# Sixteen transfers of eight partitions for part of a weight load

## The reference

```python
def expert_choice_ffn(h, router_w, wg, wu, wd):
    B, S, D = h.shape
    C = max(1, EC_CAPACITY_FACTOR * S // N_EXPERTS)          # 32 tokens per expert
    aff = jax.nn.softmax((h @ router_w).astype(jnp.float32), axis=-1)
    gate, idx = lax.top_k(jnp.swapaxes(aff, 1, 2), C)
    ...
    a = jnp.einsum('becd,edf->becf', xs, wg)                  # 1024 -> 1408
    u = jnp.einsum('becd,edf->becf', xs, wu)                  # 1024 -> 1408
    o = jnp.einsum('becf,efd->becd', jax.nn.silu(a) * u, wd) * gate[..., None]
    return jax.vmap(lambda oi, ii: jnp.zeros((S, D), h.dtype).at[ii].add(oi))(o, flat_idx)
```

## Time and profile before

| | |
|---|---|
| median of 3 runs | 1959.3 us (1957.9 to 1959.34) |
| span of the profiled execution (first to last instruction) | 1954.0 us |
| median less that span | 5.3 us |
| TensorE busy | 1562.5 us, 80% of the span |
| mean rate of the DMA engines | 330 GB/s over the span |

### The profile page before, as it was taken

The page is one execution under the profiler, slowest core; times in us unless marked ns, Lnnn a source line. Parts: engine busy times, 40 slices in busy tenths (PEclk is TensorE's granted clock), DMA queues, the critical chain, the costliest instruction groups (busy, mean ns, idle before and its releaser), DMA issues.

```text
span 1954.0 us, 22376 instructions
## 1 busy us (share of the span) xinstructions
PE 1562.5 (80%) x9738; PEld 877.7 (45%) x9738; DVE 561.0 (29%) x1102; ACT 251.6 (13%) x582; POOL 45.8 (2%) x24
## 2 busy tenths in 40 slices
PE   9999999886656675568899999998857566566767
PEld 6687688432222232223365887884313222222323
DVE  3654782211211121123335456612111111111211
ACT  3333210200000000001122432102000000000000
POOL 0300100000000000000003000000000000000000
PEclk9999999987887788789999999999988778877889
DMA  7622046699999999999972224277999999999998
GB/s 301 233 91 87 1 199 242 275 392 430 426 434 429 434 430 432 438 429 422 427 328 87 92 107 184 103 305 310 431 432 438 433 427 428 436 430 435 428 431 365
DMA packets 28221, 643.87 MB, mean 330 GB/s; under 512 B 3040, under 2 KB 4576, under 8 KB 7392
## 3 DMA queue, kind: packets, MB, share of 16 engines
q1 hardware_dynamic: 26960, 638.41, 77.5%
q10 hardware_dynamic: 1168, 4.07, 0.5%
HBM read 641.42 MB, written 1.05 MB: 329 GB/s over the span
## 4 chain that ended last, share of the span: by engine, by line
PE 51%; DMA 45%; DVE 2%; issue 1%; DVEq 1%; ACT 0%; SPq 0%; ACTq 0%
DMA region<-w_down_dram 42%; PE ps L1046 11%; PE ps L630 7%; PE ps L693 6%; PE ps L800 6%; PE ps L866 3%; PE ps L973 2%; DMA ring<-w_gbu_dram 2%; PE ps L656 2%; PE ps L783 1%; PE ps L716 1%; PE ps L671 1%; PE ps L772 1%; DMA region<-w_down_last_dram 1%; PE ps L535 1%; PE ps L598 1%
## 5 line engine op out<-in xcount | busy, mean ns | idle before, releaser
L973 PE MATMUL ps<-ring,region 128*32 128x384 f32 (+1 forms) x2842 | 288.3, 536 | 173.9 <-DMA ring<-w_gbu_dram 173.9
L1046 PE MATMUL ps<-region,late 128*32 128x512 f32 x1320 | 219.7, 790 | 146.7 <-DMA region<-w_down_dram 143.0
L973 PEld LDWEIGHTS ps<-ring,region 128*32 128x32 f32 x2842 | 117.8, 124 | 336.5 <-DMA ring<-w_gbu_dram 192.9
L1046 PEld LDWEIGHTS ps<-region,late 128*32 128x32 f32 x1320 | 57.6, 140 | 287.8 <-issue 283.6
L630 PE MATMUL ps<-xnT,ring 128*128 128x256 f32 x768 | 178.3, 380 | 4.3 <-DVE region L1429 2.6
L1811 DVE TENSOR_TENSOR region<-region,ps 128x256 f32<-128x256 f32 x32 | 13.5, 421 | 514.9 <-PE ps L973 514.9
L630 PEld LDWEIGHTS ps<-xnT,ring 128*128 128x128 f32 x768 | 140.6, 190 | 23.9 <-DVE region L1429 4.4
L1823 DVE COPY region<-ps 128x512 f32<-128x512 f32 x30 | 20.7, 692 | 344.6 <-PE ps L1046 344.6
L1070 PE MATMUL ps<-region 128*128 128x512 f32 x208 | 100.4, 615 | 19.4 <-issue 19.4
L973 PE MATMUL ps<-region 128*32 128x384 f32 (+1 forms) x1224 | 102.5, 463 | 2.2 <-DMA region<-w_ga_dram 2.2
L693 PE MATMUL ps<-xnT,ring 128*128 128x256 f32 x384 | 86.8, 380 | 0.0
(11 more groups left out here) (256 smaller groups left out, 1566.4 us busy)
## 6 DMA issues: line engine op xcount, KB each, us to landing
region<-w_down_dram SPq DMA_DIRECT2D x28, 5632.0 KB, 32.3
ring<-w_gbu_dram SPq DMA_DIRECT2D x28, 4928.0 KB, 33.3
region<-w_ga_dram SPq DMA_DIRECT2D x14, 6336.0 KB, 36.9
ring<-w_ga_dram SPq DMA_DIRECT2D x11, 6336.0 KB, 36.2
ring<-units_dram SPq DMA_DIRECT2D x26, 2048.0 KB, 8.1
region<-units_dram SPq DMA_DIRECT2D x8, 2048.0 KB, 11.7
ring<-w_ga_dram SPq DMA_DIRECT2D x2, 4288.0 KB, 20.7
ring<-w_ga_dram SPq DMA_DIRECT2D x4, 2112.0 KB, 10.6
```

The source lines that it names most:

```text
L973: m = mm(bank(b, QW[j], rows=CAP, row0=CAP * j), xs[:, i, q * CAP:(q + 1) * CAP], row[:, c0:c0 + QW[j]], start=i == 0, stop=i == DB - 1)
L1046: m = mm(bank(c, rows=CAP, row0=CAP * j), hT[:, b * P + CAP * j:b * P + CAP * (j + 1)], wd[:, CT * b + j, c * 512:(c + 1) * 512], start=b ...
```

## The change

In each layer, the last 1664 of piece 0's 2816 columns are taken out of its one transfer over 128 partitions. SyncE loads them right behind it by sixteen transfers, of eight neighbouring partitions each, all on a new semaphore `wd_rest_in`. TensorE waits for that semaphore too before it starts `last_output`. The other four pieces and everything else stay as they are.

```diff
+REST = 1664
+NARROW = 8
...
+                def load_down_rest(cols):
+                    for p0 in range(0, P, NARROW):
+                        rows = slice(p0, p0 + NARROW)
+                        sp.dma_start(R[rows, cols], w_down_last[L, rows, cols]).then_inc(s["wd_rest_in"], 16)
...
                         for b, (c0, c1) in enumerate(((0, NF_TILES), (NF_TILES, 2 * NF_TILES), (2 * NF_TILES, 3 * NF_TILES),
                                                       (3 * NF_TILES, 4 * NF_TILES - 3), (4 * NF_TILES - 3, 4 * NF_TILES))):
-                            cols = slice(c0 * QC, c1 * QC)
+                            cols = slice(c0 * QC, c1 * QC - (REST if b == 0 else 0))
                             sp.dma_start(R[:, cols], w_down_last[L, :, cols]).then_inc(wd_in[b], 16)
+                            if b == 0:
+                                load_down_rest(slice(cols.stop, c1 * QC))
...
                         if last and q == GROUP - 1:
+                            pe.wait_ge(s["wd_rest_in"], 16 * (P // NARROW) * (L + 1))
                             last_output(n)
                             return
```

More of the change, by code:

```diff
@@ L253, in build @@
         wd_last = R[:, 0:NF_TILES * D].rearrange("p (c r d) -> p c r d", c=D // QC, r=NF_TILES)
-        names = """one_dve half_dve consts_in dft_in vec_in fvec_in qkw_in filt_in decay_in wqb_in filt3_in wgbu_in wga_third_in wga_last_in wu_tail_in out_done
+        names = """one_dve half_dve consts_in dft_in vec_in fvec_in qkw_in filt_in decay_in wqb_in filt3_in wgbu_in wga_third_in wga_last_in wu_tail_in wd_rest_in out_done
         norm1_rms r_dve r2_dve xT_psum xw_dve xw_act r_psum xnT_dve lat_psum lat_rms lat_ready latT_psum latT_dve latT_act
```

## The result

The changed kernel takes 1968.67 us (median of 5 runs, 1966.88 to 1970.31), the kernel before in the same comparison 1957.9 us. The ratio is 1.0058 (95% interval 1.0048 to 1.0069): slower by 0.6%, some 11 us. The forecast was 1968.3 us from the older median of 1959.3 us, so 9.0 us. The profiled execution of after has a span of 1966.9 us and took 1968.67 us itself, 1.8 us more than its span. By the same 1.8 us the profiled execution of before took near 1955.8 us, less than its median; the two spans lie 12.9 us apart where the medians lie 10.8 us apart. I explain the 12.9 us of the two profiles.

The account below looks back on a forecast made before the run. The expert stages were taken to run at the weight stream's DMA pace. 4.0 us in each layer plus 1.0 us for the clock made 9.0 us on 1959.3 us, so 1968.3 us, range 1957.5 to 1977.0 us.

Parts of the forecast that it names:

- Eight engines for eight rows: Each narrow transfer uses the same eight DMA engines, which gain 2.04 us of work while the other eight lose 2.04 us.
- Issue cost hidden: SyncE's sixteen more issues per layer, 7.1 us, stay hidden behind the backlogged weight stream, by 3 us in layer 1.
- The crowded narrow part, T = 10 us: Eight engines aiming at eight neighbouring partitions slow each other; their narrow part takes 10 us, between bounds 4.08 and 32.6 us.
- On the leading half: The narrow part falls on the eight engines that end some 4.0 us earlier, and that lead is subtracted; chance 0.33.
- What is late: The last landing of piece loads comes 4.0 us late in each layer; in layer 0 the next layer's loads shift alike.
- The clock: Longer TensorE pauses between pieces may bring one more stretch at low clock: 1.0 us for both layers.
- no effect: Rival: narrow transfers alternate over all sixteen engines and load stays even, 1959.3 us; chance 0.09.
- even end: Rival: the leading half takes the narrow part at full speed, both halves end near 1945.2 us; time 1958.3 us, chance 0.23.
- wrong half at full speed: Rival: the narrow part falls at full speed on the lagging engines, +2.0 us in each layer, 1963.3 us; chance 0.09.
- issues bind: Rival: a narrow issue takes 1.0 us, so SyncE is late and each layer loses about 4 us, 1967.3 us; chance 0.06.
- Wrong half and crowded: Rival: T = 10 on the lagging engines, +8.0 us in each layer and +1.0 for the clock, 1976.3 us; chance 0.14.
- The case in step: Rival: eight engines stay on the same partitions throughout; 1980.3 us from T = 16 on, 2011 us at upper bound; chance 0.06.

Follow-up runs that it names:

- issues-alone run: The changed kernel with its sixteen narrow transfers carrying 8 columns, not 1664, the rest going over 128 partitions: 1960.3 us, ratio 1.0016 to the kernel before.
- load-alone run: The kernel before plus, in layer 1, eight extra transfers into partitions 0 to 63, rows four apart, into a tile nobody reads: 1958.89 us, ratio 1.001.
- layer 1 alone: The changed kernel with the change made in layer 1 only, layer 0 as in the kernel before: 1964.43 us, ratio 1.0037.
- sixteen slices: The changed kernel with the 1664 columns cut into sixteen transfers of 104 columns, each over all 128 partitions: 1959.82 us, ratio 1.0014.

## Why the prediction was right, and where it was not

- **Eight engines for eight rows:** right, by the 256 small packets more.
- **Issue cost hidden:** right. They take 5.5 to 5.7 us, not 7.1, and end long before the backlog does. Completions at "nothing, under 0.3 us" was wrong, and no row stood behind that term: the issues-alone run costs 3 us over both layers.
- **The crowded narrow part, T = 10 us:** the mechanism was right in its pattern, that engines slow each other on neighbouring partitions: runs with equal bytes and equal load show it. That the partitions' write side is the cause is argued. What I had as one effect is two: neighbours on one path, and the crossing into the other engines' half. The second I had not seen at all. T was never measured by itself. Its parts of which runs tell something are 4.08 us at full speed and some 1.6 us for sixteen transfers' overhead; the slowed packets come on top. By the windows the stream loses more than T = 10 us would make it: (10 - 4.08) / 2 = 3.0 us of all sixteen engines were forecast for a layer, and 13 us at 219 in place of 418 GB/s are 6.2 us in layer 1, 9 us at 255 GB/s are 3.5 us in layer 0 (estimates).
- **On the leading half:** only partly. By the shares of the load-alone run the eight engines are a mixture, six that lead and two that are late, so the lead of 4.0 us that I took off is not there for all.
- **What is late:** this step failed, and the sum did not show it. I had the narrow part delay only what is queued behind it: pieces 0 to 4, 4.0 us in each layer. But the slowed paths belong to all sixteen engines, and some of these still carry the tail of `w_gbu` when others have begun the narrow rows. That is how I read it; the profile doesn't show packets by engine. So a transfer ahead of the change lands some 2.2 us (layer 0) and 3.1 us (layer 1) late, and TensorE's up product, not the down tiles, meets the delay first. And what holds up the end of layer 1 is not the last landing, as I had it, but piece 1, with three quarters of TensorE's closing work still to come. In layer 0 that and the low clock are the whole 3.8 us; my 4.0 us was right by its size alone.
- **The clock:** 1.0 us for both layers was too small. The row of 24 matmuls takes 4.06 us in layer 0, 1.9 us more than the 2.14 us at full clock, and of the 2.8 us that the two down groups in layer 1 lose, 1.4 us lie on the path.
- **Layer 1:** 4.0 us plus part of the clock was forecast, 8.9 us came in the profile, 7.3 us in the run with layer 1 alone. The profile's 12.9 us is in part the fast execution of before; against the medians, layer 0 has some 3.5 us and layer 1 some 7.3 us. The total of 9.0 us came out near 10.8 us because delays that I had charged to the pieces stood in for ones that I had not listed.
- **The absolute time:** that 1968.3 us met 1968.67 us so closely is luck. The forecast span of 1963.0 us was 3.9 us short of 1966.9 us, and the 5.3 us from span to median, which I took to stay, were 1.8 us.

Of the rivals, no effect, even end and wrong half at full speed are refuted by the rate of 219 GB/s, and issues bind by the 0.34 to 0.36 us of an issue. Wrong half and crowded, at 1976.3 us, would have cost more; by the mixture of six and two it is not the case, but not wholly false either. The case in step would have cost more too (its upper bound adds up to 2013 us, not 2011).

## What to carry to other kernels

Cut a load along its columns, over all 128 partitions, not into groups of partitions, and keep the pieces few (one more cost nothing, sixteen cost 3 us). A group of eight keeps half of the engines off the work, and eight or sixteen neighbours at a time bring the rate to 219 and 246 GB/s, which slows even a transfer that was issued before. Look at GB/s beside the busy share of the DMA engines: a full share with little over half of the rate was the sign of it here. It is no proof by itself, since small packets lower the rate too (340 GB/s at a full share in the issues-alone run). Where one half of the engines ends early, rows moved to it would still have to be written into the late half's partitions; I expect no gain from that, but no run had exactly the leading eight.

## What the runs showed that I had not expected

- Eight extra transfers of equal bytes cost 2 us in partitions 0 to 63 and 7 us in 64 to 127 (1.001 and 1.0035).
- A narrow transfer of next to no bytes costs each of its engines about 0.1 us, an estimate from the issues-alone run's window.
- An issue of eight partitions in a row takes SyncE 0.34 us, one of eight partitions with a step 0.68 us (2.73 and 5.45 us for eight).
- In the changed kernel one issue in layer 1 takes 5.51 us, where others take 0.45. Layer 0 has none such. It is the last of the four, for piece 4, and ends at 1935.4 us, long before TensorE needs that piece, so I put no cost on it. The runs issues alone and layer 1 alone have it too (7.53 and 7.42 us for the last four issues), and the sixteen slices have three long ones in a row in each layer; what holds them is open.

```profile
1929.93 5.51 SPq L442 DMA_DIRECT2D region<-w_down_last_dram  x1
```
